# Two norms taken from raw halves of the residual, head sums in column tiles, and a reordered tail in a two-layer hybrid decoder kernel

## The chip, the cores and the metric

The kernel runs on one core of a Trainium2 chip. The metric is the device time of one execution in microseconds (us), lower is better. Time before: median of three runs.

## What is computed

Two decoder layers over 256 positions of width 1024, all in float32. What matters here, cut from the reference:

```python
def rmsnorm(x, g, eps=RMS_EPS):
    y = x * lax.rsqrt(jnp.mean(x * x, axis=-1, keepdims=True) + eps)
    return y * g

h = h + even_mixer(rmsnorm(h, ln_mix[0]), ...)        # norm 0
h = h + swiglu(rmsnorm(h, ln_ffn[0]), ...)            # norm 1
gate = sigmoid(rmsnorm(h, ln_ple[0]) @ w_ple_gate[0]) # norm 2
h = h + gate * (p[0] @ w_ple_proj[0])
hn = rmsnorm(h, ln_mix[1])                            # norm 3
proj = hn @ w_in_odd                                  # q, k, v, z, b, a
qkv = silu(causal_dwconv(qkv, conv_w))                # 4 taps
q, k = l2norm(q), l2norm(k)                           # per head of 128
beta, g = sigmoid(b), -exp(a_log) * softplus(a + dt_bias)
o = chunk_gated_delta_rule(q, k, v, g, beta)          # chunks of 64
h = h + (rmsnorm(o, onorm_g) * silu(z)) @ w_out
h = h + moe_swiglu(rmsnorm(h, ln_ffn[1]), ...)        # top 2 of 8
```

After the experts come a second gate stage and the final norm.

## The kernel before

One program for the whole trunk, with the order of every engine's work written out by hand and semaphores between the engines. Weights stream in pieces of 128x2048 float32 (1 MB): SyncE loads a piece into one of six `raw` slots, ScalarE (ACT) rounds it to `w_hi` (`split`, L1355), VectorE (DVE) forms the rest `w_lo` (L1906), and TensorE (PE) multiplies in three products, high by high, high by low, low by high (`product`, L593 to L595). Activations are split the same way into `xs_hi` and `xs_lo`. `w_hi` and `w_lo` have three slots, so the split of a piece waits until the third last one is used. `splits(n)` and `ahead_to(n)` in a program mean: split all pieces up to n here; everything behind such a call on that engine waits for it.

A norm (0 to 3) goes: ACT squares and sums the residual `h` and takes the root (`norm_std`, L1374, L1375), DVE takes the reciprocal and writes the scaled `hn` (`norm_hn`, L1924, L1925), PE transposes the 16 blocks of `hn` (`norm_x`, L656), ACT and DVE split them with the gain (`norm_hi` L1384, `norm_lo` L1930), and the following products start.

Around norm 2, PE finishes the down projection of the dense SwiGLU, runs `proj` for the embedding (24 matmuls), waits for norm 2 (`norm_x(2)`), and runs the gate matmuls (four pieces, 96 matmuls of 512 columns, `tokens_out`). ACT applies the sigmoid (L1524), DVE multiplies and adds to `h` (L2149, L2089), and norm 3 follows in the same way. Then comes the DeltaNet layer: `small_product` (L834) and `small_turn` (L843) for b and a; twelve pieces of q, k, v (`qkv`, 48 matmuls of 256 columns each, alternating between PSUM banks 0 and 1). ACT copies each bank into the padded `upo` (`pad`, L1558), DVE applies the four taps (`conv`, L2180 and L2182), ACT the SiLU. `decay_sums` (L932), `gram`, `x_first` and five levels of a block inversion (`level_p`, `level_x`, all L942) run between the pieces. `square` (ACT, L1550) and `l2_sum` (PE, L896: matmuls with one column, four for each of two heads and two token tiles, eight such calls with four matmuls each) give the squared norms of q and k; DVE's `head_squares` (L2198) reads them. Small results of PE share banks 2 and 3 in the order of the list `SIDE`; a step may start when the one two places ahead has been read (`side_bank`).

At the end of the inversion come `corner`, `z_unit` (12 matmuls of 512 columns each), u (L1057), w (L1062, read by ACT as `nwT`, L1654), `scores` (L918), the state (L1071), the outputs, the per-head norm (`head_squares` and `head_roots` on ACT, L1668 and L1672; `head_factors` and `head_scale` on DVE, L2371 and L2364), the transposes `heads_turn` (L1111), and the output projection (`P_OUT_O`), which reads them split by `heads_hi` (L1686) and `heads_lo` (L2390). Then router, experts (four pairs or more of 84 pieces each), last gate and final norm.

## Time and profile before

| | |
|---|---|
| median of 3 runs | 1662.44 us (1661.19 to 1668.97) |
| the profiled execution's own time | 1666.08 us |
| its span, first to last instruction | 1664.3 us |
| mean granted TensorE clock | 0.986 |
| busy PE / DVE / ACT | 1610.2 / 1321.5 / 1058.8 us |
| HBM read | 447.75 MB |

The trace has every instruction with its start, its length, and the engine that ended the idle time before it. Ends of matmuls are modelled, so lengths of one matmul overlap; starts are what to go by. The granted clock is the share of full speed (2.4 GHz) that TensorE was given: 1.00 or 0.50 (1.2 GHz), and values between where a stretch has both.

### The profile page before, as it was taken

The numbers are of one execution on the slowest core, as the hardware profiler recorded it, in microseconds if no ns is written. First come the engines' busy times: TensorE is split into PE (matmuls) and PEld (weight loads), VectorE is DVE, ScalarE is ACT, GpSimd is POOL, SyncE is SP. The second block draws the span as 40 slices with busy tenths as digits, with TensorE's granted clock in tenths as the row PEclk, the third lists the DMA queues.
The fourth block names the chain that finished last, engine by engine and source line by source line (L and its number), as shares of the span: only waits on it lengthen the run. The fifth ranks groups of instructions, "written<-read, shape, count | busy, mean of one in ns | idle before, by whom it ended". The sixth has DMA issues, their size and how long they took to land.

```text
span 1664.3 us, 21969 instructions
## 1 busy us (share of the span) xinstructions
PE 1610.2 (97%) x9012; PEld 1359.4 (82%) x9012; DVE 1321.5 (79%) x1175; ACT 1058.8 (64%) x940; POOL 28.4 (2%) x24
## 2 busy tenths in 40 slices
PE   7988999997999989999999999999999999999997
PEld 6977888886999877788888888888888888888885
DVE  5766666666687568888989889889889888889886
ACT  5554344336543258677777777777777777777777
POOL 0000000000131100000000000000000000000000
PEclk9999999999989999999999999999999999999999
DMA  9634555544323236999999999999999998999991
GB/s 299 205 104 158 203 177 202 178 152 127 102 79 102 76 138 210 336 367 372 359 367 326 369 363 381 347 377 326 371 376 369 356 368 302 380 366 358 362 372 41
DMA packets 220191, 450.22 MB, mean 271 GB/s; under 512 B 10270, under 2 KB 58300, under 8 KB 220092
## 3 DMA queue, kind: packets, MB, share of 16 engines
q1 hardware_dynamic: 219404, 447.78, 75.2%
q8 instruction: 71, 1.16, 0.3%
q10 hardware_dynamic: 688, 1.05, 0.2%
q14 instruction: 28, 0.23, 0.0%
HBM read 447.75 MB, written 1.05 MB: 270 GB/s over the span
## 4 chain that ended last, share of the span: by engine, by line
PE 89%; DVE 6%; ACT 3%; issue 1%; DMA 0%; SPq 0%; ACTq 0%; DVEq 0%
PE ps L593 24%; PE ps L594 23%; PE ps L595 23%; PE ps L774 6%; PE ps L776 3%; DVE w_lo L1906 2%; PE ps L942 2%; PE ps L637 1%; ACT w_hi L1355 1%; DVE odd L2182 1%; PE ps L896 0%; DVE h L2089 0%; ACT L1367 0%; PE ps L1214 0%; PE ps L1180 0%
## 5 line engine op out<-in xcount | busy, mean ns | idle before, releaser
L1906 DVE TENSOR_TENSOR w_lo<-raw,w_hi 128x2048 fp32r<-128x2048 f32 x421 | 960.6, 2297 | 192.5 <-ACT w_hi L1355 192.1
L1355 ACT ACTIVATE w_hi<-raw 128x2048 fp32r<-128x2048 f32 x421 | 806.4, 1917 | 226.7 <-PE ps L595 221.7
L593 PE MATMUL ps<-w_hi,x_both 128*128 128x512 f32 x1096 | 438.2, 400 | 14.5 <-DVE x_both L1930 8.2
L595 PE MATMUL ps<-w_hi,x_both 128*128 128x512 f32 x1096 | 430.7, 393 | 0.0
L594 PE MATMUL ps<-w_lo,x_both 128*128 128x512 f32 x1096 | 429.5, 392 | 0.0
L593 PEld LDWEIGHTS ps<-w_hi,x_both 128*128 128x128 f32 x1096 | 207.9, 190 | 59.8 <-issue 8.0
L595 PEld LDWEIGHTS ps<-w_hi,x_both 128*128 128x128 f32 x1096 | 207.3, 189 | 44.8
L594 PEld LDWEIGHTS ps<-w_lo,x_both 128*128 128x128 f32 x1096 | 208.2, 190 | 41.3
L594 PE MATMUL ps<-w_lo,ff 128*128 128x512 f32 x576 | 226.4, 393 | 0.0
L593 PE MATMUL ps<-w_hi,ff 128*128 128x512 f32 x576 | 226.2, 393 | 0.0
L595 PE MATMUL ps<-w_hi,ff 128*128 128x512 f32 x576 | 224.6, 390 | 0.0
L774 PE MATMUL ps<-x_both,w_hi 128*128 128x512 f32 x448 | 159.1, 399 | 0.4 <-DVE x_both L1930 0.4
L593 PEld LDWEIGHTS ps<-w_hi,ff 128*128 128x128 f32 x576 | 108.2, 188 | 24.3
L595 PEld LDWEIGHTS ps<-w_hi,ff 128*128 128x128 f32 x576 | 108.2, 188 | 23.9
L594 PEld LDWEIGHTS ps<-w_lo,ff 128*128 128x128 f32 x576 | 108.3, 188 | 21.7
L776 PE MATMUL ps<-x_both,w_lo 128*128 128x256 f32 x448 | 125.8, 281 | 0.0
L774 PEld LDWEIGHTS ps<-x_both,w_hi 128*128 128x128 f32 x448 | 84.2, 188 | 21.7 <-issue 0.6
L776 PEld LDWEIGHTS ps<-x_both,w_lo 128*128 128x128 f32 x448 | 84.7, 189 | 0.5
L593 PE MATMUL ps<-x_both,w_hi 128*128 128x256 f32 x288 | 84.9, 295 | 0.0
L594 PE MATMUL ps<-x_both,w_hi 128*128 128x256 f32 x288 | 82.5, 287 | 0.0
L595 PE MATMUL ps<-x_both,w_lo 128*128 128x256 f32 x288 | 82.4, 286 | 0.0
L1764 ACT ACTIVATE ff<-ps,ff 128x512 f32<-128x512 f32 x56 | 38.5, 688 | 41.8 <-PE ps L595 41.8
(332 smaller groups left out, 1262.5 us busy)
## 6 DMA issues: line engine op xcount, KB each, us to landing
raw<-in_w_moe SPq DMA_DIRECT2D x336, 1024.0 KB, 6.7
raw<-in_w_dense SPq DMA_DIRECT2D x42, 1024.0 KB, 5.0
raw<-in_w_in_odd SPq DMA_DIRECT2D x16, 1024.0 KB, 5.5
raw<-in_w_in_even SPq DMA_DIRECT2D x12, 1024.0 KB, 10.8
raw<-in_w_ple_gate SPq DMA_DIRECT2D x8, 1024.0 KB, 6.5
raw<-in_w_out_even SPq DMA_DIRECT2D x4, 1024.0 KB, 5.9
raw<-in_w_out_odd SPq DMA_DIRECT2D x4, 1024.0 KB, 5.0
raw<-in_w_ple_proj SPq DMA_DIRECT2D x2, 1024.0 KB, 4.8
```

The costliest lines, as they stand in the source:

```text
L593: pe.matmul(acc, lh, rh, start=first, stop=False)
L594: pe.matmul(acc, lh, rl, start=False, stop=False)
L595: return pe.matmul(acc, ll, rh, start=False, stop=final)
L637: last = pe.transpose(ps[:, bank, c * P:(c + 1) * P], src[:, c * P:(c + 1) * P], ident)
L774: pe.matmul(ps[:, 2 * m + c, :], wh[:, k, c * P:(c + 1) * P], x_both[:, k * 2 * SEQ:(k + 1) * 2 * SEQ], start=(k == 0), stop=False)
L776: last = pe.matmul(ps[:, 2 * m + c, 0:SEQ], wl[:, k, c * P:(c + 1) * P], xs_hi[:, k, :], start=False, stop=(k == KC - 1))
L942: last = pe.matmul(ps[rows, bank, cols], lhs(rows, hd, cols), rhs(rows, hd, cols), start=True, stop=True)
L1355: act.activation(w_hi[:, n % SPLIT, :], raw[:, slot, :], ACT.Copy).then_inc(hi_rdy, 1)
L1764: act.activation(sil[:, s % 2, :], ps[:, 2 * (s % 2), :], ACT.Silu, scale=gslot[:, u, 1:2]).then_inc(silu_sb, 1)
L1906: dve.tensor_tensor(w_lo[:, n % SPLIT, :], raw[:, slot, :], w_hi[:, n % SPLIT, :].bitcast(F32), ALU.subtract).then_inc(lo_rdy, 1)
L2182: last = dve.scalar_tensor_tensor(qkvT[:, ch, :], src, tap, qkvT[:, ch, :], ALU.mult, ALU.add)
```

## The change

1. **Norms 2 and 3.** PE transposes raw `h` in two halves of 512 columns (`turn_h`), the gain is applied in the split as before, and 1/rms is applied to the products. For norm 2 it is the `scale` of the sigmoid. For norm 3 it is a row `rb` (two matmuls broadcast `rstd` over the partitions, ACT copies it) that multiplies q, k, v as they leave PSUM, the `scale` of the SiLU of z, and a factor on b and a. ACT sums squares by halves (`half_square`), DVE adds eps (`half_eps`), `half_root` and `half_rstd` follow. `norm_std`, `norm_hn` and `norm_x` for these two are gone.
2. **Order around them.** The last down projection runs half by half (`mlp_half`), residual adds follow each half, `proj` is cut in two around the transposes, the gate's last piece runs behind `turn_h(3, 0)`, and the first q, k, v pieces start with the lower half of the inputs.
3. **Convolution.** `pad` goes from ACT to DVE (PSUM times `rb`), the first tap from DVE to ACT (`tap`).
4. **Squared sums.** Four calls for four heads each instead of eight for two: four matmuls with a stationary 128x32 of ones, each into 32 partitions of its own, 256 columns; ACT copies the result (`l2_out`), two transposes (`l2_turn`), DVE reads.
5. **Tail.** In the corner stage the split of `P_QKV_O + 15` moves behind the w copies on ACT; piece 17's split moves behind the second `head_roots` and `head_scale`; `heads_turn(1)` moves between the two token tiles of the first output piece.

```diff
@@ PE, last down projection and norm 2
-                for c in range(2):
-                    for t in range(NT):
-                        at = c * SEQ + t * P
-                        for half in range(2):
+                for half in range(2):
+                    for c in range(2):
+                        for t in range(NT):
+                            at = c * SEQ + t * P
...
+                    if s == HALF_FJ - 1 and half == 0:
+                        last.then_inc(mlp_half, 1)
...
-            norm_x(2)
+            pe.wait_ge(h_ready, H_AT[2][0])
+            turn_h(2, 0)
+            proj_e(0)
+            pe.wait_ge(h_ready, H_AT[2][2])
+            turn_h(2, 1)
+            proj_e(1).then_inc(piece_used, 1)
...
+            for j, half, t in ((0, 0, 0), (0, 0, 1), (0, 1, 0), (0, 1, 1)):
+                gate_e(j, half, t)
+            first(2, KC - 1)
+            gate_e(1, 0, 0)
+            gate_e(1, 0, 1)
+            pe.wait_ge(h_ready, H_AT[3][0])
+            turn_h(3, 0)
+            gate_e(1, 1, 0)
+            gate_e(1, 1, 1)
@@ PE, start of the DeltaNet layer
-            qkv(0)
+            split_wait(P_QKV_O)
+            pe.wait_ge(h_ready, H_AT[3][1])
+            small_product(3, 2, x_both, wba_s, 4 * HEADS_D, small_ps, range(0, 4))
+            qkv_part(0, 0, range(0, 4))
+            pe.wait_ge(sgm_sb, 2 * NT)
+            turn_h(3, 1, (0,))
+            pe.wait_ge(h_ready, H_AT[3][2])
+            turn_h(3, 1, (1,))
+            split_wait(P_QKV_O + 1)
+            qkv_part(1, 0, range(0, 4))
+            qkv_part(0, 0, range(4, KC))
+            small_product(3, 2, x_both, wba_s, 4 * HEADS_D, small_ps, range(4, KC))
+            qkv_part(0, 1, range(KC)).then_inc(piece_used, 1)
+            pe.wait_ge(rs_rdy, 2 * NT)
+            for t in range(NT):
+                last = pe.matmul(ps[:, 6, t * P:(t + 1) * P], rstd[:, 3, t:t + 1].broadcast_to([P, P]), ident,
+                                 start=True, stop=True)
+            last.then_inc(rb_ps, 1)
             pe.wait_ge(small_sb, 1)
             small_turn(0, 7, 4 * HEADS_D, C_S16, smallT_ps)
@@ PE, squared sums
-            def l2_sum(i):
-                bank = side_bank(("l2", i))
-                pe.wait_ge(l2_sq, i % 8 + 1 + (4 if i >= 8 else 0))
-                for t in range(NT):
-                    for c in range(2):
-                        last = pe.matmul(ps[:, bank, 2 * t + c:2 * t + c + 1],
-                                         sq[:, i % 2, c * SEQ + t * P:c * SEQ + (t + 1) * P], ones[:, 0:1],
-                                         start=True, stop=True)
+            def l2_sum(u):
+
+                bank = side_bank(("l2", u))
+                pe.wait_ge(l2_sq, 2 * u + 2)
+                if u == 0:
+                    pe.wait_ge(d_exp, 4)
+                for c in range(4):
+                    last = pe.matmul(ps[32 * c:32 * c + 32, bank, 0:SEQ], ones[:, 0:32],
+                                     squares_of(u)[c // 2][:, (c % 2) * SEQ:(c % 2 + 1) * SEQ], start=True, stop=True,
+                                     tile_position=(0, 32 * c))
+                last.then_inc(l2_ps, 1)
...
             qkv(4)
             l2_sum(0)
+            gram(0)
+            l2_turn(0)
             l2_sum(1)
-            gram(0)
-            l2_sum(2)
-            l2_sum(3)
             gram(1)
+            l2_turn(1)
@@ ACT, convolution and corner stage
-            def pad(i):
-
-                act.wait_ge(piece_used, P_QKV_O + i + 1)
-                if i >= 4:
-                    act.wait_ge(cv_done, i - 3)
-                act.activation(upo[:, i % 4, :, DN_TAPS - 1:], ps[:, i % 2, :].rearrange("p (c s) -> p c s", c=2),
-                               ACT.Copy).then_inc(q_pad, 1)
+            def tap(i):
+
+                act.wait_ge(q_pad, i + 1)
+                for m in range(2):
+                    ch = 2 * QKV_ORDER[i] + m
+                    last = act.activation(qkvT[:, ch, :], upo[:, i % 4, m, 0:SEQ], ACT.Copy, scale=cwT[:, ch:ch + 1])
+                last.then_inc(tap_sb, 1)
@@ DVE, convolution
+            def pad(i):
+
+                dve.wait_ge(piece_used, P_QKV_O + i + 1)
...
+                dve.tensor_tensor(upo[:, i % 4, :, DN_TAPS - 1:], ps[:, i % 2, :].rearrange("p (c s) -> p c s", c=2),
+                                  over(rb, 2), ALU.mult).then_inc(q_pad, 1)
@@ PE, first output piece
-            tokens_out((6, 7), (xs_hi, xs_lo), P_OUT_O, 0, ready_k=heads_in)
-            heads_turn(1)
+            for t in range(NT):
+                for k in range(4):
+                    heads_in(k)
+                    last = product(ps[:, 6 + t, :], (xs_hi[:, k, t * P:(t + 1) * P], xs_lo[:, k, t * P:(t + 1) * P]),
+                                   (wh[:, k, :], wl[:, k, :]), k == 0, False)
+                if t == 0:
+                    heads_turn(1)
```

How the order moves, at three places. The first is DVE behind the last down projection: before,

```order
L2130 TENSOR_TENSOR ff<-ps,ff 128x512 [waits pT_hi]
L1906 TENSOR_TENSOR w_lo<-raw,w_hi 128x2048 [waits hi_rdy]
L2089 TENSOR_TENSOR h<-h,ps 128x512 [waits piece_used]
L2089 TENSOR_TENSOR h<-h,ps 128x512 x3
L1924 RECIPROCAL rstd<-std 128x1 [waits n_std,h_ready]
L1925 TENSOR_SCALAR hn<-h,rstd 128x1024 [waits dve_link]
L1924 RECIPROCAL rstd<-std 128x1 [waits n_std]
L1925 TENSOR_SCALAR hn<-h,rstd 128x1024 [waits dve_link]
L1906 TENSOR_TENSOR w_lo<-raw,w_hi 128x2048 [waits hi_rdy] x2
```

and in the change:

```order
L2254 TENSOR_TENSOR ff<-ps,ff 128x512 [waits pT_hi]
L2030 TENSOR_TENSOR w_lo<-raw,w_hi 128x2048 [waits hi_rdy]
L2213 TENSOR_TENSOR h<-h,ps 128x512 [waits mlp_half]
L2213 TENSOR_TENSOR h<-h,ps 128x512
L2030 TENSOR_TENSOR w_lo<-raw,w_hi 128x2048 [waits hi_rdy]
L2213 TENSOR_TENSOR h<-h,ps 128x512 [waits piece_used]
L2213 TENSOR_TENSOR h<-h,ps 128x512
L2054 SCALAR_TENSOR_TENSOR x_both<-ps,gT,x_both 128x256 [waits n_hi] x4
```

Two of the four residual adds now come earlier than before, and a weight split stands between the two pairs. The second place is ACT in the corner stage (corner copies L1595 and L1716, squares L1550 and L1663, w copies L1654 and L1779): before,

```order
L1595 ACTIVATE raw<-ps 64x8x64 [waits corner_ps]
L1565 ACTIVATE odd<-odd 128x512 [waits cv_done]
L1550 ACTIVATE odd<-odd 128x512 [waits cv_silu,side_ps]
L1595 ACTIVATE raw<-ps 64x8x64 [waits corner_ps]
L1355 ACTIVATE w_hi<-raw 128x2048 [waits piece_used,raw_in2]
L1654 ACTIVATE odd<-ps 128x512 [waits w_ps] x2
L1565 ACTIVATE odd<-odd 128x512 [waits cv_done]
L1550 ACTIVATE odd<-odd 128x512 [waits cv_silu,side_ps]
```

and in the change:

```order
L1716 ACTIVATE raw<-ps 64x8x64 [waits corner_ps]
L1685 ACTIVATE odd<-odd 128x512 [waits cv_done]
L1716 ACTIVATE raw<-ps 64x8x64 [waits corner_ps]
L1663 ACTIVATE odd<-odd 128x512 [waits cv_silu,l2_ps]
L1685 ACTIVATE odd<-odd 128x512 [waits cv_done]
L1663 ACTIVATE odd<-odd 128x512 [waits cv_silu,l2_ps]
L1671 ACTIVATE s<-ps 128x256 [waits side_ps,l2_ps]
L1779 ACTIVATE odd<-ps 128x512 [waits w_ps] x2
L1434 ACTIVATE w_hi<-raw 128x2048 [waits piece_used,raw_in2]
```

The last squares move ahead of the w copies and the weight split behind them; on DVE the matching `w_lo` still stands ahead of the last `head_squares`. The third place is ACT at the head norms (roots L1672 and L1796): before,

```order
L1672 ACTIVATE osd<-oss 128x8 [waits od_sum]
L1668 ACTIVATE odd<-odd 128x1024 [waits od_sb]
L1355 ACTIVATE w_hi<-raw 128x2048 [waits piece_used,raw_in0]
L1672 ACTIVATE osd<-oss 128x8 [waits od_sum]
L1367 ACT_TABLE_LOAD
L1367 ACTIVATE eps<-eps 128x1
```

and in the change:

```order
L1796 ACTIVATE osd<-oss 128x8 [waits od_sum]
L1792 ACTIVATE odd<-odd 128x1024 [waits od_sb]
L1796 ACTIVATE osd<-oss 128x8 [waits od_sum]
L1446 ACT_TABLE_LOAD
L1446 ACTIVATE eps<-eps 128x1
L1434 ACTIVATE w_hi<-raw 128x2048 [waits piece_used,raw_in0,act_link]
```

The second root no longer has a weight split ahead of it, and the split follows the table load.

## Rows read from the trace of the kernel before

**Rows 1.** The page: busy time of each engine, and the costliest groups on DVE and ACT

```profile
PE 1610.2 (97%) x9012; PEld 1359.4 (82%) x9012; DVE 1321.5 (79%) x1175; ACT 1058.8 (64%) x940; POOL 28.4 (2%) x24
...
L1906 DVE TENSOR_TENSOR w_lo<-raw,w_hi 128x2048 fp32r<-128x2048 f32 x421 | 960.6, 2297 | 192.5 <-ACT w_hi L1355 192.1
L1355 ACT ACTIVATE w_hi<-raw 128x2048 fp32r<-128x2048 f32 x421 | 806.4, 1917 | 226.7 <-PE ps L595 221.7
```

**Rows 2.** Waits of PE from 300 to 700 us: total, times, longest

```profile
PE ps L656 <- DVE hn L1925: 5.3, 1, 5.3
PE ps L593 <- DVE x_both L1930: 4.2, 1, 4.2
PE ps L1111 <- DVE odd L2364: 3.1, 1, 3.1
PE ps L896 <- DVE yneg L2198: 2.1, 1, 2.1
PE ps L896 <- ACT odd L1550: 2.0, 1, 2.0
PE ps L834 <- DVE x_both L1930: 1.6, 1, 1.6
...
PE ps L593 <- DVE x_both L2390: 1.2, 1, 1.2
```

**Rows 3.** Windows: length, busy PE, PEld, DVE, ACT, POOL (instructions), granted clock, DMA share, GB/s

```profile
385.00:388.00 3.00, 3.00 (x9) 2.35 (x8) 2.97 (x3) 0.00 (x0) 0.00 (x0) 0.50 0.85 291
...
461.00:469.00 8.00, 8.00 (x61) 7.87 (x61) 5.17 (x12) 2.08 (x3) 1.83 (x2) 0.50 0.46 131
566.00:571.00 5.00, 5.00 (x23) 5.00 (x24) 1.10 (x4) 0.00 (x0) 1.01 (x1) 0.50 0.56 204
598.00:602.00 4.00, 1.11 (x9) 1.13 (x10) 2.71 (x6) 0.84 (x3) 0.00 (x0) 1.00 0.32 76
680.00:800.00 120.00, 120.00 (x543) 98.95 (x543) 106.96 (x63) 89.19 (x58) 0.00 (x0) 1.00 1.01 369
```

**Rows 4.** Timeline around norm 2: start us, length us, engine, line, operation, [idle before <-releaser]

```profile
369.01 2.29 DVE L1906 TENSOR_TENSOR w_lo<-raw,w_hi 128x2048 fp32r<-128x2048 f32 x1 [1.11 <-ACT w_hi L1355]
372.07 2.48 DVE L2089 TENSOR_TENSOR h<-h,ps 128x512 f32<-128x512 f32 x4 [0.77 <-PE ps L595]
...
377.37 1.80 PE L656 MATMUL ps<-con,hn 128*128 128x128 f32 x15
...
379.81 3.00 ACT L1384 ACTIVATE x_both<-ps,gT 128x256 fp32r<-128x256 f32 x8
```

**Rows 5.** Timeline on ACT at the end of the two gate halves, and behind them

```profile
396.35 1.09 ACT L1524 ACTIVATE hn<-ps 128x512 f32<-128x512 f32 x2 [2.01 <-PE ps L595]
...
407.23 1.09 ACT L1524 ACTIVATE hn<-ps 128x512 f32<-128x512 f32 x2 [3.43 <-PE ps L595]
408.33 1.28 ACT L1367 ACT_TABLE_LOAD   x1
```

**Rows 6.** Timeline, opening of the DeltaNet layer, up to the first level of the inversion

```profile
427.10 0.28 PE L843 MATMUL ps<-con,odd 32*128 32x16 f32 x1
...
439.90 0.60 ACT L1558 ACTIVATE odd<-ps 128x512 f32<-128x512 f32 x1 [3.36 <-PE ps L595]
...
440.45 2.71 DVE L2182 SCALAR_TENSOR_TENSOR odd<-odd,cwT 128x256 f32<-128x256 f32 x6
...
455.68 1.84 PE L896 MATMUL ps<-con,odd 128*128 128x1 f32 x16
...
478.86 1.10 PE L942 MATMUL ps<-odd 64*64 64x64 f32 x32
```

**Rows 7.** Timeline, corner stage: the second w copy on ACT, and the state's start on PE

```profile
563.49 0.60 ACT L1654 ACTIVATE odd<-ps 128x512 f32<-128x512 f32 x1 [0.30 <-PE ps L1062]
...
574.22 1.95 PE L1071 MATMUL ps<-odd 128*128 128x128 f32 x16
```

**Rows 8.** Timeline, head norms: the second root on ACT

```profile
597.04 0.19 ACT L1672 ACTIVATE osd<-oss 128x8 f32<-128x8 f32 x1
```

More of the change, by code:

```diff
@@ L1608, in _ @@
             act.activation(dcy[:, :, :, :], dcy[:, :, :, :], ACT.Exp).then_inc(dcy_rdy, 1)
-            decay(0, 0)
-            decay(0, 1)
-            pad(3)
-            decay(1, 0)
-            decay(1, 1)
+            for t in range(NT):
+                for g in range(2):
+                    decay(t, g)
             silu_conv(0)
             square(0)
+            tap(3)
             silu_conv(1)
```

352 lines of the change are left out of this document (221 added, 131 removed).

## The prediction

> **What bounds the kernel now.** I read the page first: PE is busy 97% of the span, DVE 79%, ACT 64% [rows 1]. So time can come only from PE: its waits, its slow-clock stretches, and work taken off it. The windows say that from 680 us on, in the experts, PE works every microsecond at full clock [rows 3]. The change touches nothing there, so the question is how much earlier PE reaches that stage. The waits of PE between 300 and 700 us say what can be won before it: 5.3 and 1.6 us at norm 3, 4.2 at norm 2, 2.1 and 2.0 at squared sums, 3.1 and 1.2 at the head norms, 19.5 us together [rows 2]. The windows add a second loss. Behind most of these waits PE was granted 0.50, which is 1.2 GHz, for a while: 3 us behind norm 2's, 8 us behind the first squared sums' and 5 us behind the last's [rows 3]. Work runs at half speed there, so these three cost 1.5, 4 and 2.5 us. Behind the 3.1 us wait the clock stayed at 1.00 [rows 3]: a wait does not always bring it down.
>
> **The change part by part.** I walk PE through the new order with durations of the rows and compare the time at five places with the time before. Units: a weight split is 1.9 us on ACT and 2.3 on DVE [rows 1]; 12 gate matmuls are 2.7, from 48 between the two sigmoids, 10.9 us [rows 5]; a transposed block is 0.12, so eight are 1.0 [rows 4]; a q, k, v piece is 5.85, from two of them between the turn that starts at 427.1 and takes 1.0, and 439.8 [rows 6]; a residual add is 0.62 [rows 4].
>
> *Norm 2.* Removed from the path: root, reciprocal, scaling and all 16 transposes between the last add and the split. Added: waits of PE for the adds. The down projection ends at about 372.0. The first two adds need its first half (over by 369.3) and DVE, which is free at 371.3 [rows 4], so they end at 372.6: PE waits 0.6, transposes until 373.6, and runs half of `proj` until 376.3. The second two adds stand behind a weight split on DVE, and that behind ACT, which first does two half squares (1.4, an estimate: 1024 columns at the rate of the 2048-column copy, and two reads of a sum) from 372.0 and then the split until 375.4. DVE splits until 377.7 and adds until 379.0. So PE waits 2.7 us, a new wait where there was none; then transposes (380.0), the other half of `proj` (382.8), gate. The gate started at 383.5 before (transposes from 377.4, 1.9, and the 4.2 us wait [rows 2, 4]): gain 0.7. Next is the second gate piece: ACT splits the inputs (0.38 a block [rows 4]) until 381.4, loads a table (1.3 [rows 5]), takes roots, splits the weights until 385.4, DVE until 387.7; PE wants it at 388.3. It is hidden by 0.6 us only.
>
> *Gate and norm 3.* Eight groups of 2.7 and the eight transposes in between end at 405.8, against 407.1 before: gain 1.3, of which 1.5 is the slow stretch that I leave out here. PE then waits for the product of the second sigmoid: ACT splits a piece until 403.6, DVE until 405.9, then sigmoid product and add, 407.3: a wait of 1.5. From there the lower halves of b, a and of two pieces cover the last transposes and splits, and the root comes after them. PE is at the small turn at 417.9 and waits for ACT (weight split, copy of `rb`, small copy) until 419.1. Before it was there at 427.1 [rows 6]: **gain 8.0**. With the parts of piece 1 already done, piece 2 starts at 424.8, not 433.9: 9.1.
>
> *Opening of the DeltaNet layer.* The decay gate comes 7.5 us earlier, at 424.0, through the same short chain with one more factor. From there DVE's chain to the third convolution is as long as before: `conv` loses two of its eight instructions (under 0.9 us) and keeps six at 2.7 [rows 6], `pad` adds one pass of 0.7 over 512 columns from PSUM, and a memset of 0.9 leaves. The tap on ACT has no row; a 128x256 block from PSUM is 0.38 [rows 4] and a 2048-column copy scaled down is 0.24, so two are 0.5 to 0.8. I take 0.8, since PSUM blocks are the nearer size. Queued behind `pad` on DVE are the weight splits, and behind `tap` on ACT its own: each pad waits for a DVE that is splitting. PE's next piece needs its bank freed, and in my walk it is, by 2 to 3 us each time. After piece 4 (446.5) PE waits 0.4 for squares and 1.6 for the fourth SiLU (449.1); the DVE chain then lets `x_first` start at 459.5 and level 1 at 464.8, against 478.9 [rows 6]: **gain 14.1**, with no slow clock in it.
>
> *Squared sums.* Eight calls fall away; two of them take 1.84 [rows 6], so 7.4 us. Four calls of four matmuls with 256 columns come, with two transposes each (0.24). No row has column tiles. A float32 matmul is two instructions, 128 columns of it 0.24; 256 columns are 0.46, four in turn 1.84, four side by side 0.46. The row of 64x64 tiles has 32 instructions of 64 columns in 1.1 us, 0.035 each [rows 6], where a transpose's rate would give 0.06, so tiles do overlap: I take 0.6 a call. Two calls were in the levels: 1.84 less 0.84, **gain 1.0** (bounds: 1.1 and a loss of 0.2).
>
> The Trainium skill ("TensorEngine Tiling (Array Packing)", Key Properties) says that different tiles can load and multiply in parallel, but also that a change of the tiling mode drains the engine. The first half agrees with the row of 64x64 tiles; the second speaks against this change, which enters and leaves column tiles four times. By the drain and no overlap the levels would lose 0.2 us instead of winning 1.0; no row here shows a drain.
>
> *Corner stage.* The 2.0 us wait for the last squares goes, with the slow 5 us behind it and 1.8 of work against 0.8. But the weight split now stands behind the w copies on ACT. These end at 564.1 [rows 7], about 563.6 in the same frame with the work saved. The split ends on ACT at 565.5 and on DVE at 567.8, and only then may `head_squares` read the sums, for which the second `scores` waits through its bank: 568.2. PE had come there at 564, so it waits 4 us: the late split is what comes last next. Scores (1.0) and a z unit (2.8) follow, the state starts at 572.0 instead of 574.2 [rows 7]: **gain 2.2**.
>
> *Head norms.* The second root starts at 597.0 [rows 8], and the split next to it kept DVE from the factor until 599.4 (ACT's part ends at 597.1, DVE's 2.3 later). Without it the root is at 596.4 and the factor at 596.8, 2.6 us earlier: the 3.1 us wait shrinks to 0.5. The split comes to lie ahead of `heads_hi` and `heads_lo`, which makes PE wait 1.1 before the first output piece. `heads_turn(1)` inside that piece removes the wait of 1.2. **Gain 2.6.**
>
> *Sum:* 14.1 + 1.0 + 2.2 + 2.6 = 19.9 us at full clock. New waits of 2.7, 1.5, 1.6 and 4 us remain; most like them were followed by a slow clock [rows 3]. I take three such stretches, at 3, 4 and 5 us long (the rows have 3, 8 and 5, but ACT and DVE cover part where they are the later ones), 6.0 us. That leaves 13.9. The profiled execution took 1666.1, so it would take 1652.2; its 1666.1 is 3.6 above the median of the runs, and against the median of 1662.4 the forecast is **1648.5 us**.
>
> **The rivals.**
> A. *The clock stays up*, as it did behind the 3.1 us wait. Then the 19.9 come whole: 1642.5. Against it: three other waits of 2 to 4 us. Chance 0.18.
> B. *The waits only move.* Splits queued ahead of adds, pads and sums make DVE and ACT the bound. From the small turn's 8.0 on nothing more is won in the opening, the slow clock costs 3.4 around the gate and the corner is even; the head norms keep 1.3: about 6 us, 1656.5. For it: three places with slack under 1 us in my walk, and DVE at 79%. Chance 0.20.
> C. *The levels lose their pace; slower.* `pad` now stands on DVE ahead of the `update` that the next level waits for. If DVE falls over 2 us a level behind, PE waits in each of five levels, and each wait brings about 8 slow microseconds like those at 461 us [rows 3], 4 us lost: 5 x 6 = 30 less 14, so 1678. Against it: a level takes PE some 13 us, and DVE gets only 0.1 more per level. Chance 0.05.
> D. *The experts don't start earlier.* Their loads run at 1.01 of the DMA engines [rows 3]; were they the bound, an earlier PE would wait there: 1662. Against it: PE has no gap from 680 on, and the loads are released by the splits, which move with PE. Chance 0.05.
>
> **How the numbers follow.** The forecast with its 13.9 holds 0.52. A measurement of this kernel tells 0.5%, 8.3 us, from no change. Faster by more: forecast, A and a fifth of B, 0.74. Within: the rest of B and D, 0.21. Slower: C, 0.05. The range 1641 to 1659 holds A, the forecast with a tap, a tile or a slow stretch at its other bound, and most of B; outside lie C, D and the edge of B, some 0.15.
>
> **What would show it.** In the new profile: L656's 5.3 us wait and the two waits at L896 gone; waits of 2 to 3 us at the second half's transposes of norm 2 and of about 4 at the second scores; the small turn near 419, level 1 near 465 to 468; column tile calls of 0.5 to 1 us; experts of unchanged length. I am wrong if level 1 is not at least 8 us earlier, if the levels take longer than before, or if the slow clock takes over 10 us in the stage.

## The result, and the profile after

| | before | after |
|---|---|---|
| median of the runs made together, 6 each | 1662.78 us (1661.03 to 1668.97) | 1654.75 us (1651.40 to 1655.37) |
| the profiled execution's own time | 1666.08 us | 1651.40 us |
| its span | 1664.3 us | 1649.6 us |
| mean granted clock | 0.986 | 0.989 |

The ratio is 0.994, with a 95% interval from 0.9924 to 0.9957. The forecast was 1648.5 with a range of 1641 to 1659: faster, as measured, but by 13.9 us where the medians give 8.0. The two profiled spans lie 14.7 apart, which looks like the forecast come true. It is not quite that: before's profiled execution is 3.3 us above the median of these runs and after's is the fastest of its six, and, as the experiments show, 3.2 us of the 14.7 come from an address, which the prediction did not see at all.

In the changed kernel the code has new line numbers: the products are L601 to L603 (before L593 to L595), `w_lo` L2030, `w_hi` L1434, `turn_h` L654, `add_h` L2213, `small_product` L869, the squared sums L941 and their transposes L951, `gram` and levels L995, `scores` L971, DVE's `head_squares` L2344, `pad` L2335, `conv` L2316, `xt_first` L2393, the heads' transposes L1183. The page after, to be read beside [rows 1]: PE lost 12.9 us of busy time, DVE 5.7.

```profile
PE 1597.3 (97%) x8992; PEld 1347.8 (82%) x8992; DVE 1315.8 (80%) x1164; ACT 1065.9 (65%) x964; POOL 27.3 (2%) x24
```

The waits of PE from 300 to 700 us, in total, times, longest, beside [rows 2]. The 5.3 us at L656 and both at L896 are gone (0.7 is left at L941, which does the squared sums now), and of the 3.1 at the heads 0.3 is left. New are 3.8 at the second scores, 2.5 at the second half's transposes (the prediction had 4 and 2.7), 1.5 at b and a (L869; the prediction had 1.5 there), three shorter ones at `gram`, `x_first` and level 1 (L995), and a wait for a DMA:

```profile
PE ps L971 <- DVE yneg L2344: 3.8, 1, 3.8
PE ps L654 <- DVE h L2213: 3.5, 3, 2.5
PE ps L995 <- DVE odd L2393: 1.8, 1, 1.8
PE ps L995 <- ACT odd L1685: 1.7, 1, 1.7
...
PE ps L869 <- issue: 1.5, 1, 1.5
PE ps L768 <- DMA ff<-in_ln_final: 1.3, 1, 1.3
...
PE ps L995 <- ACT odd L1705: 0.7, 1, 0.7
```

How early PE is at the places of the prediction, from the timelines. The forecast column has the sum at full clock; the 6.0 us for the slow clock were to come off at the end.

| place | before, us | forecast, us | after, us | earlier by | forecast gain |
|---|---|---|---|---|---|
| gate of norm 2 | 383.5 | 382.8 | 384.5 | -1.0 | 0.7 |
| small turn | 427.1 | 419.1 | 420.8 | 6.3 | 8.0 |
| level 1 | 478.9 | 464.8 | 471.0 | 7.8 | 14.1 |
| state | 574.2 | 556.9 | 565.4 | 8.8 | 17.3 |
| router's sums (L1165, now L1244) | 639.7 | 625.8 with the slow clock | 629.8 | 9.9 | 13.9 |
| end of the span | 1664.3 | | 1649.6 | 14.7 | 13.9 |

So PE reached the router 4 us later than forecast, and 4.8 us more of gain appeared behind it, in a part that was to stay as it was. The windows tell where the clock was down (columns as in [rows 3]; the lost time of a window is 10 us times what its clock lacks to 1.00). Of the kernel before:

```profile
380.00:390.00 10.00, 6.52 (x22) 5.24 (x23) 7.97 (x11) 4.61 (x9) 0.00 (x0) 0.83 0.46 118
410.00:420.00 10.00, 5.99 (x23) 3.93 (x23) 7.89 (x15) 7.46 (x15) 0.00 (x0) 0.77 0.29 79
420.00:430.00 10.00, 10.00 (x74) 9.72 (x74) 0.62 (x4) 2.93 (x5) 0.00 (x0) 0.89 0.17 61
460.00:470.00 10.00, 9.29 (x66) 9.16 (x67) 7.17 (x15) 3.08 (x3) 2.83 (x2) 0.50 0.37 105
560.00:570.00 10.00, 7.98 (x52) 7.82 (x52) 4.61 (x6) 4.23 (x5) 0.01 (x1) 0.78 0.40 140
570.00:580.00 10.00, 10.00 (x59) 8.90 (x58) 2.08 (x3) 1.19 (x2) 4.67 (x4) 0.88 0.00 0
660.00:670.00 10.00, 7.79 (x31) 5.92 (x30) 9.52 (x26) 6.16 (x5) 0.00 (x0) 0.90 0.70 245
670.00:680.00 10.00, 10.00 (x42) 8.13 (x41) 7.88 (x6) 5.75 (x3) 0.00 (x0) 0.93 0.98 352
```

That is 15.2 us. After, the windows below 1.00 from 370 to 680 us hold 6.8:

```profile
370.00:380.00 10.00, 6.89 (x34) 5.31 (x34) 7.11 (x8) 6.00 (x12) 0.00 (x0) 0.95 0.00 0
380.00:390.00 10.00, 10.00 (x44) 8.42 (x43) 5.38 (x13) 9.00 (x14) 0.00 (x0) 0.88 0.01 3
...
450.00:460.00 10.00, 8.85 (x111) 7.78 (x112) 6.28 (x15) 6.90 (x10) 1.62 (x2) 0.83 0.01 2
460.00:470.00 10.00, 8.20 (x99) 7.74 (x99) 9.90 (x11) 1.42 (x3) 5.99 (x3) 0.83 0.36 107
560.00:570.00 10.00, 9.83 (x57) 8.98 (x58) 2.95 (x7) 1.19 (x2) 3.46 (x3) 0.83 0.34 105
```

The 1.7 us lost before at 660 to 680 are one part of what appeared behind the router. The rest is found in the last experiment.

### The profile page after: what moved, and what is told of

It reads as the page before. It is cut to its first block, busy times and chain, and to the rows that moved or that the text cites. A ratio compares the mean times of both kernels' runs of the same rounds, so it can differ in the third digit from the quotient of the medians.

```text
span 1649.6 us, 21944 instructions
## 1 busy us (share of the span) xinstructions
PE 1597.3 (97%) x8992; PEld 1347.8 (82%) x8992; DVE 1315.8 (80%) x1164; ACT 1065.9 (65%) x964; POOL 27.3 (2%) x24
## 4 chain that ended last, share of the span: by engine, by line
PE 84%; DVE 8%; ACT 5%; issue 2%; DMA 1%; SPq 0%; ACTq 0%; DVEq 0%
PE ps L601 22%; PE ps L603 22%; PE ps L602 22%; PE ps L782 6%; DVE w_lo L2030 4%; PE ps L784 3%; PE ps L995 2%; ACT w_hi L1434 2%; PE ps L645 1%; ACT L1446 1%; DVE h L2213 0%; DMA ff<-in_ln_final 0%; DVE odd L2316 0%; PE ps L1293 0%; ACT x_both L1463 0%
## 5 line engine op out<-in xcount | busy, mean ns | idle before, releaser
L2030 DVE TENSOR_TENSOR w_lo<-raw,w_hi 128x2048 fp32r<-128x2048 f32 x421 | 960.7, 2297 | 195.3 <-ACT w_hi L1434 194.9
L1434 ACT ACTIVATE w_hi<-raw 128x2048 fp32r<-128x2048 f32 x421 | 806.4, 1917 | 211.8 <-PE ps L603 208.6
L601 PE MATMUL ps<-w_hi,x_both 128*128 128x512 f32 x1096 | 437.3, 399 | 10.6 <-DVE x_both L2054 4.2
L603 PE MATMUL ps<-w_hi,x_both 128*128 128x512 f32 x1096 | 429.8, 392 | 0.0
L601 PEld LDWEIGHTS ps<-w_hi,x_both 128*128 128x128 f32 x1096 | 207.4, 189 | 55.3 <-issue 6.7
L603 PEld LDWEIGHTS ps<-w_hi,x_both 128*128 128x128 f32 x1096 | 206.9, 189 | 44.5
L601 PE MATMUL ps<-w_hi,ff 128*128 128x512 f32 x576 | 225.9, 392 | 0.0
L603 PE MATMUL ps<-w_hi,ff 128*128 128x512 f32 x576 | 224.8, 390 | 0.0
L603 PEld LDWEIGHTS ps<-w_hi,ff 128*128 128x128 f32 x576 | 108.3, 188 | 23.0
L601 PEld LDWEIGHTS ps<-w_hi,ff 128*128 128x128 f32 x576 | 108.5, 188 | 22.4
L601 PE MATMUL ps<-x_both,w_hi 128*128 128x256 f32 x288 | 84.6, 294 | 0.1
L603 PE MATMUL ps<-x_both,w_lo 128*128 128x256 f32 x288 | 82.0, 285 | 0.0
L1888 ACT ACTIVATE ff<-ps,ff 128x512 f32<-128x512 f32 x56 | 38.6, 689 | 41.2 <-PE ps L603 41.2
```

Source lines behind the costliest of these rows:

```text
L601: pe.matmul(acc, lh, rh, start=first, stop=False)
L603: return pe.matmul(acc, ll, rh, start=False, stop=final)
L1434: act.activation(w_hi[:, n % SPLIT, :], raw[:, slot, :], ACT.Copy).then_inc(hi_rdy, 1)
L1888: act.activation(sil[:, s % 2, :], ps[:, 2 * (s % 2), :], ACT.Silu, scale=gslot[:, u, 1:2]).then_inc(silu_sb, 1)
L2030: dve.tensor_tensor(w_lo[:, n % SPLIT, :], raw[:, slot, :], w_hi[:, n % SPLIT, :].bitcast(F32), ALU.subtract).then_inc(lo_rdy, 1)
```

## The experiments

All were timed beside the kernel before, in four sets, and a ratio is to the kernel before of the same set. Its median was 1664.14 us in the first set (after_again, sums_first, adds_first, before_filled), 1663.54 in the second (both_first, level_first, tail_only, before_filled2), 1663.28 in the third (level_first2, tail_first, best2) and 1664.47 in the fourth (before_shift). A ratio comes from all executions and can differ a little from that of the two medians. after_again, level_first, level_first2 and tail_first lie within each other's intervals, so the times do not tell these four apart and only the profiles do; sums_first and adds_first, timed in the same set as after_again, just touch its interval, and both_first and best2 are clear of it.

| run | base | median us | ratio | 95% interval |
|---|---|---|---|---|
| after_again | changed | 1652.58 | 0.9929 | 0.9915 to 0.9944 |
| sums_first | changed | 1647.82 | 0.9904 | 0.9886 to 0.9922 |
| adds_first | changed | 1648.27 | 0.9914 | 0.9897 to 0.9931 |
| both_first | changed | 1643.30 | 0.9871 | 0.9856 to 0.9887 |
| level_first | changed | 1650.23 | 0.9917 | 0.9904 to 0.9930 |
| level_first2 | changed | 1651.82 | 0.9931 | 0.9918 to 0.9945 |
| tail_first | changed | 1651.01 | 0.9924 | 0.9910 to 0.9938 |
| best2 | changed | 1636.81 | 0.9853 | 0.9839 to 0.9866 |
| before_filled | before | 1664.60 | 1.0001 | 0.9991 to 1.0010 |
| before_filled2 | before | 1661.07 | 0.9980 | 0.9971 to 0.9988 |
| tail_only | before | 1662.43 | 0.9986 | 0.9975 to 0.9997 |
| before_shift | before | 1662.17 | 0.9983 | 0.9972 to 0.9994 |

**The changed kernel once more (after_again).**

> The changed kernel once more, beside the kernel before on the same chip. Theory 1 (waits and slow clock): in the two profiled executions the change took 14.7 us off, of which 8.4 is slow clock that happened to differ (lost to half speed in 10 us windows: 21.4 us before, 15.3 after, over the whole span; 15.2 and 6.8 from 370 us on). So the medians differ by less than the profiles: 6 to 11 us, ratio 0.9935 to 0.996, and the time lost to the slow clock in a new profile is 8 to 16 us. Theory 2 (the experts start no earlier in most executions): the medians differ by under 5 us, and the end of the new profile lies under 8 us ahead of the old one.

The same kernel gave 1652.58 here and 1654.75 in the runs of the result; its waits are the same to 0.1 us, while its profiled execution lost 10.2 us to the slow clock from 370 to 680 us, not 6.8. So the waits repeat and the clock does not: two profiles of one kernel lie 3.4 us apart there by the clock alone. The following runs on the changed kernel are held against 1652.6.

**The squares' wait in the corner (sums_first).** DVE reads the last squared sums ahead of the split, not behind it:

```diff
@@ DVE, corner stage
-            ahead_to(15)
             head_squares(3)
+            ahead_to(15)
```

> The changed kernel, but DVE reads the last squared sums before it splits the piece whose high part now comes late. Theory 1 (the 3.8 us wait at the second scores is the DVE order, and costs in full): the wait is gone, the state starts 3.8 to 5.5 us earlier (5.5 with the slow clock behind it), median 3 to 6 us under the changed kernel's. Rival (the late weight split itself then holds the z units): the wait goes to a z unit, median within 1.5 us of the changed kernel's.

The corner of the changed kernel, PE and then DVE (start us, length us): the sums are in PSUM at 555.4, but DVE waits 4.3 us for ACT's half of the split, splits until 559.9 and only then reads them. This is the wait that the prediction had walked out, down to its size.

```profile
555.05 0.38 PE L951 MATMUL ps<-con,s 128*128 128x128 f32 x2
555.27 1.06 PE L971 MATMUL ps<-odd 128*128 128x128 f32 x8
560.17 2.08 PE L971 MATMUL ps<-odd 128*128 128x128 f32 x8 [3.84 <-DVE yneg L2344]
```

```profile
557.68 2.29 DVE L2030 TENSOR_TENSOR w_lo<-raw,w_hi 128x2048 fp32r<-128x2048 f32 x1 [4.29 <-ACT w_hi L1434]
559.89 0.22 DVE L2344 TENSOR_SCALAR yneg<-ps 128x4 f32<-128x4 f32 x2
```

In sums_first DVE reads them at 553.07 and the scores run through; from the small turn to the state PE takes 139.2 us instead of 144.6. The median fell by 4.8 us: the wait of 3.8 and about 1 us of the slow clock behind it (the 560 window is at 0.83 above, which is 1.7 us in that one execution, and at 1.00 in sums_first).

```profile
552.87 1.95 PE L971 MATMUL ps<-odd 128*128 128x128 f32 x16
```

**The adds' wait at norm 2 (adds_first).** DVE adds the second halves of the residual ahead of the split of the gate piece:

```diff
@@ DVE, norm 2
-            splits(P_GATE_E)
             dve.wait_ge(piece_used, P_PROJ_E)
             for t in range(NT):
                 add_h(t, 1, ps[:, 5 + 2 * t, :]).then_inc(h_ready, 1)
+            splits(P_GATE_E)
```

> The changed kernel, but DVE does the second pair of residual adds of norm 2 before the weight split. Theory 1 (the 2.5 us wait before the second half's transposes is the split that stands ahead of the adds): that wait is gone and the gate starts 3 to 4 us earlier; about 1 us comes back as a wait for the second gate piece, whose split follows the norm on ACT; median 2 to 3.5 us under the changed kernel's. Rival (the weight split of the second gate piece becomes the bound): the gain is under 1 us.

After: the second transposes wait 2.47 us and then run at half speed (1.97 us for what takes 1.07 in the row above it). In adds_first they start at 376.87 without a wait, the gate starts at 380.5 instead of 384.5, and a wait of 0.47 us comes at the second gate piece, the one that the prediction had as covered by 0.6 us only. 4.3 us less in all.

```profile
373.11 1.07 PE L654 MATMUL ps<-con,h 128*128 128x128 f32 x8 [0.64 <-DVE h L2213]
379.40 1.97 PE L654 MATMUL ps<-con,h 128*128 128x128 f32 x8 [2.47 <-DVE h L2213]
```

**Both together (both_first).**

> The changed kernel with both reorderings of the two runs before it: DVE reads the last squared sums ahead of the split of piece 15, and adds the second residual halves of norm 2 ahead of the split of the gate piece. Alone they measured 4.8 and 4.3 us under the changed kernel. Theory 'two waits in series, each paid in full': 1652.6 - 4.8 - 4.3 = 1643.5 us (1642 to 1645). Rival 'the time gained at norm 2 is taken back by the squares' wait or by the loads': the better of the two alone, 1647.8 us.

1643.3 us, where 1643.5 was expected: two waits in series on PE, each paid in full.

**Filling the waits of the kernel before (before_filled, before_filled2).** PE runs matmuls that nothing reads while it waits at norm 3, at the third squared sums and at the last ones, so that the engine is not idle ahead of the stretches with the slow clock. They add work to the program and take none away.

```diff
+            def fill(bank, n):
+                for _ in range(n):
+                    pe.matmul(ps[:, bank, :], ident, con[:, 0:512], start=True, stop=True)
...
+            pe.wait_ge(h_ready, H_AT[3][0] - 1)
+            fill(0, 11)
...
+            pe.wait_ge(d_exp, 4)
+            fill(6, 4)
...
+            pe.wait_ge(u_sb, 2)
+            fill(4, 4)
```

> The kernel before, with matmuls that nothing reads put into three waits of TensorE: 11 of 128x512 float32 before the transposes of norm 3, 4 before the third squared sum, 4 before the last one. Nothing else is changed, and no wait gets shorter. Theory 1 (the slow clock comes from the waits and costs half the time it lasts): the granted clock stays at 1.00 behind these three waits, and the kernel gains what they cost in the profile, 3.4 + 5 + 3.4 less what another engine takes back, 5 to 11 us. Rival (the clock falls for another cause, such as the kind of work): no gain, or a loss of up to 1 us.

The fills were too long: one of these matmuls takes 0.87 us, so 11 of them took 9.6 us in a wait of 5.3, and 4 of them 3.5 in waits of 2.1 and 2.0. The clock did stay at 1.00 in all three stretches, and the median was that of the kernel before (ratio 1.0001). In the profiled execution the sum closes: about 12 us less of slow clock up to 680 us (3.4 against 15.2), some 7 us of overrun, and the router's sums 5.0 us earlier. But this execution, at 1661.15 us, was the fastest of twelve, and the median shows no such gain. With 5, 2 and 2 of them:

> The kernel before with unread matmuls in the same three waits as the filled kernel before it, now 5, 2 and 2 of them, at 0.87 us each 4.4, 1.7 and 1.7 us, which is no more than the waits last. Theory 'the slow clock behind the waits costs': the granted clock stays at 1.00 in the three stretches, and the 12 us that the profile of the kernel before loses there (3.4 at 404 to 430, 5 at 460, 3.4 at 560 to 580) come back as far as the executions timed have them too: 5 to 12 us under 1664.1, so 1652 to 1659. Rival 'behind a slow PE the others catch up, so full speed only lengthens the next wait': 0 to 2 us, 1662 to 1664. Third case: the clock falls in spite of the fills, since they are float32 and short, and the time is 1664.

Here the fill at norm 3 takes 4.45 us and fits. The result lies between the theories: 1661.07, a ratio of 0.9971 to 0.9988, so 2.0 to 4.8 us, where 5 to 12 were expected. The clock was not kept up everywhere; in this profile it was down at the norm 2 wait, which had no fill, and again behind two of the fills:

```profile
380.00:390.00 10.00, 5.94 (x16) 4.75 (x17) 8.56 (x11) 5.20 (x10) 0.00 (x0) 0.66 0.41 112
410.00:420.00 10.00, 6.24 (x27) 2.97 (x25) 7.85 (x14) 8.48 (x17) 0.00 (x0) 0.97 0.31 89
420.00:430.00 10.00, 10.00 (x68) 8.90 (x68) 1.80 (x8) 1.94 (x3) 0.00 (x0) 0.85 0.28 93
460.00:470.00 10.00, 9.81 (x84) 8.55 (x83) 9.02 (x16) 4.07 (x5) 3.71 (x3) 0.83 0.38 107
```

So the slow clock does cost time, some microseconds, but not each microsecond that one profile shows as lost. How much of it belongs to a given wait these runs do not settle.

**The opening of the levels (level_first, level_first2).** Level 1 came 6.2 us later than forecast. The first run takes DVE's `xt_first(0)` ahead of a split and ACT's copy `x_first(0)` ahead of `tap(5)`, which had held ACT for 8.6 us; the second moves `x_first(1)` there as well.

```diff
@@ DVE
-            ahead_to(6)
             xt_first(0)
+            ahead_to(6)
             xt_first(1)
@@ ACT (level_first2; level_first moves only the first copy)
+            x_first(0)
+            x_first(1)
             tap(5)
-            x_first(0)
             ahead_to(8)
             silu_conv(4)
-            x_first(1)
```

> The changed kernel; at the opening of the levels DVE makes the first transposed block (xt_first(0)) ahead of the split of piece 6, and ACT copies the first product (x_first(0)) ahead of tap(5), which had to wait 8.6 us for a pad that stands behind a convolution. Theory 'order of the opening': PE's 1.8 us wait before x_first(0) and its 0.7 us wait before level 1 go, and with them about 1.5 us lost in the slow clock behind the first; level 1 starts at 467 instead of 471.0, and the kernel takes 1649 to 1650 (3 to 4 us under 1652.6). Rival 'DVE beside GpSimd': DVE's six instructions of conv(4) take 4.7 us instead of 2.7 while GpSimd's masks run, so everything behind them on DVE stays where it is, PE waits in level 1 instead and the time is 1652 to 1653.

> The run level_first once more, with ACT's second copy (x_first(1)) ahead of tap(5) as well. In level_first PE's wait before x_first(0) was gone, but a wait of 2.1 us came before the second half of level 1, released by the copy of x_first(1), which had stood behind tap(5) and a split on ACT. Theory 'ACT's queue': that wait goes too, 1650.2 - 2.1 = 1648.1 us, the state starts about 2 us earlier than the 563.8 of level_first. Rival 'DVE is the bound of the opening, behind GpSimd's masks': the wait comes back under DVE's name in the first level, 1650 us.

The first median, 1650.2, is where the first theory had it, and the theory is wrong all the same. In that profile the state comes 145.1 us behind the small turn, no sooner than after's 144.6; what is earlier is the small turn itself, by 2.1 us, at a place that the edit does not touch. The named waits go, but 2.1 us come back at the second half of level 1, and when that copy is moved too, 0.98 and 1.00 come back in the levels and 0.76 at a split; that run has 1651.8, slower and not 2.1 faster.

In level_first2 level 1 starts 47.0 us behind the small turn instead of 50.2, the end of the levels (L1104) 116.1 instead of 117.1, and the state 144.6, as after. So of the 3.2 us won at level 1 some 2.2 are given back in the levels, and the last 1.0 in a longer slow stretch behind the corner's wait (the windows at 550 and 560 are at 0.84 and 0.82, after at 1.00 and 0.83). What gives them back is seen on ACT: the level's copy (L1711), for which PE waits, stands behind a tap and a split, and the tap waited 4.04 us for DVE's `pad`. ACT, then PE:

```profile
478.10 0.91 ACT L1678 ACTIVATE odd<-odd,cwT 128x256 f32<-128x256 f32 x2 [4.04 <-DVE odd L2335]
478.92 1.89 ACT L1434 ACTIVATE w_hi<-raw 128x2048 fp32r<-128x2048 f32 x1
480.72 0.57 ACT L1711 ACTIVATE odd<-ps 128x512 f32<-128x512 f32 x1
```

```profile
481.44 3.01 PE L995 MATMUL ps<-odd 64*64 64x64 f32 x96 [1.00 <-ACT odd L1711]
```

And DVE had little room to come sooner: it is busy 28.0 of 30 us in the changed kernel (24.4 in the same window of the kernel before, 26.4 from 463 to 493 us, around its own first levels), and 29.1 in level_first2. That DVE sets the pace here is read from these rows and not shown by a run of its own, and an order of ACT with these taps behind the level's copies was not tried. After, then level_first2:

```profile
455.00:485.00 30.00, 27.46 (x424) 26.29 (x421) 28.04 (x39) 15.67 (x19) 10.23 (x6) 0.94 0.36 107
```

```profile
455.00:485.00 30.00, 27.26 (x447) 26.10 (x447) 29.13 (x40) 15.25 (x20) 10.77 (x7) 1.00 0.36 107
```

Part of that busy time is stretch. Where GpSimd (POOL) masks the blocks, DVE's instructions stretch, and GpSimd's too. After, DVE's conv(4) takes 4.74 us for six instructions and the next one 3.62, against 2.71 in [rows 6]; GpSimd's mask takes 3.24 us beside DVE's split, and 1.30 two microseconds earlier beside a DVE product with one operand in PSUM. DVE first, then POOL:

```profile
457.49 1.38 DVE L2382 TENSOR_TENSOR raw<-ps,odd 64x512 f32<-64x512 f32 x2
...
464.00 4.74 DVE L2316 SCALAR_TENSOR_TENSOR odd<-odd,cwT 128x256 f32<-128x256 f32 x6
```

```profile
457.65 1.30 POOL L2007 TENSOR_TENSOR odd<-raw,con 128x512 f32<-128x512 f32 x1 [28.12 <-DVE raw L2388]
459.68 3.24 POOL L2007 TENSOR_TENSOR odd<-raw,con 128x512 f32<-128x512 f32 x1 [0.72 <-DVE raw L2388]
463.55 3.07 POOL L2007 TENSOR_TENSOR odd<-raw,con 128x512 f32<-128x512 f32 x2 [0.63 <-DVE odd L2393]
```

The Trainium skill ("SBUF — State Buffer", Who interferes with whom) says that a DVE instruction with two SBUF inputs contends with a GpSimd one that reads SBUF, and one with at most one SBUF input, outside DVE's 2-port modes, does not. The trace agrees with both halves, by the 4.74 and the 1.30 us. The kernel before had the same collision (there two first taps, L2180, take 2.68 us beside a mask, against 0.35 for one alone at 452.69 us), but behind a `qkv` piece at half speed, where PE waited for none of it. No run keeps the masks and DVE apart, so what the collision costs the changed kernel is not shown.

**The heads (tail_only, tail_first).** The change's order at the head norms alone, in the kernel before:

```diff
@@ ACT and DVE
-            ahead_to(17)
             head_roots(1)
             load_table(ACT.Silu)
+            ahead_to(17)
...
-            ahead_to(17)
             head_factors(1)
             head_scale(1, 0)
+            ahead_to(17)
@@ PE: heads_turn(1) between the two token tiles of the first output piece
```

> The kernel before with nothing but the change's order at the head norms: piece 17's split behind the second root and head_scale, heads_turn(1) between the two token tiles of the first output piece. Theory: 2.6 us of PE's waits of 3.1 and 1.2 go, 1664.1 - 2.6 = 1661.5 us, ratio 0.998; the second heads' waits in the profile are 0.3 to 0.5. Rival 'the split's 2.3 us come back ahead of the output piece': 1663.5 to 1664.1.

1662.43 us, 1.1 below by the medians; the ratio, 0.9986, gives 2.3, with an interval of 0.5 to 4.2. The profile splits it: from the state to the heads' transposes 24.0 us instead of 26.7, the 2.7 gained as predicted; from there to the router's sums 40.4 instead of 38.8, so 1.6 is lost again. The 1.2 us ahead of an output piece have only moved, and a wait for the load of `p_tok` is new:

```profile
594.69 1.06 PE L1111 MATMUL ps<-con,odd 128*128 128x128 f32 x8 [0.34 <-DVE odd L2371]
599.72 0.47 PE L593 MATMUL ps<-w_hi,x_both 128*128 128x512 f32 x1 [1.20 <-DVE x_both L2397]
613.10 0.66 PE L760 MATMUL ps<-con,ff 128*128 128x128 f32 x4 [1.29 <-DMA ff<-in_ln_final]
```

That row names `in_ln_final`, which ACT loads right behind `p_tok` and with the same semaphore. ACT issues both once DVE has split the last heads. PE now reaches its use sooner, the load does not. tail_first repairs both in the changed kernel:

```diff
@@ ACT
             heads_hi(1)
-            act.wait_ge(odT_lo, 4)
             act.dma_start(p_tok[:, :, :], a["p"][1, 0].rearrange("(t p) d -> p t d", p=P)).then_inc(p_in, 16)
             act.dma_start(gfin[:, :], a["ln_final"].unsqueeze(0).broadcast_to([P, D])).then_inc(p_in, 16)
+            act.wait_ge(odT_lo, 4)
@@ DVE
-            ahead_to(17)
             heads_lo(0)
             head_scale(0, 1)
             head_scale(1, 1)
-            ahead_to(18)
+            ahead_to(17)
             heads_lo(1)
+            ahead_to(18)
```

> The changed kernel with two repairs at the head norms: DVE rounds the first heads (heads_lo(0)) and the second ones ahead of the splits of pieces 17 and 18, and ACT issues the load of p_tok right behind heads_hi(1) instead of behind DVE's last heads_lo. Theory: the change's order moved the second transposes ahead but left the load where it was relative to DVE, so the 1.3 us that PE waits for it is new, and the 1.2 us before the first output piece are the split's; both go: 1652.6 - 2.4 = 1650.2 us, and from heads_turn to the gather 41.3 us instead of 43.7. Rival 'the splits that now come later, or the loads themselves, take their place': 1652.6 us and 43.7.

Both waits are gone and heads to gather takes 41.2 us, as expected. The median fell by 1.6 to 1651.0, less than 2.4; by time alone it is not clear of after_again (0.9910 to 0.9938 against 0.9915 to 0.9944).

**Everything together (best2).**

> All reorderings together on the changed kernel: squares ahead of a split, adds ahead of a split, the opening of the levels as in level_first2, the heads as in tail_first. If the waits stand in series and each is paid in full: 1643.3 - 4.5 (opening) - 2.4 (heads) = 1636.4 us. If the opening's gain is taken back once the corner no longer waits for the squares: 1641.

1636.81 us, ratio 0.9853 (0.9839 to 0.9866): 15.8 us better than the changed kernel (after_again) and 26.5 better than the one before. Its opening window:

```profile
455.00:485.00 30.00, 27.25 (x493) 25.93 (x493) 29.18 (x35) 12.21 (x18) 10.15 (x7) 1.00 0.38 110
```

DVE is as full here as in level_first2. The median is where the theory had it, but the theory's 4.5 us for the opening is not what the profiles show. The span is 8.0 us shorter than both_first's. Of these 1.5 are there before the gate of norm 2, where the two kernels are the same; 2.4 are the heads', from the state to the gather; 1.5 lie behind the gather, where both_first alone had a slow stretch (its 620 window is at 0.83). The other 2.7 lie between the small turn and the state (139.2 and 136.5 us). 1.7 of them is a slow stretch of both_first at 460 to 480 us, which followed a wait of 2.2 us for ACT's `x_first` copy (L1705) that best2 does not have. So the order of the opening gave between 1.0 and 2.7 us here, where in level_first2 it had given nothing by the state. With one profile of each, more cannot be said.

**An address (before_shift).** What remained was 3 us in the experts. The mean lengths of their matmuls differ in a group that the change does not touch, the down projection, whose stationary operand is a tensor of the expert stage (`ff`); of their operands it is the only one that stands behind the changed buffers in the order of allocation. From 700 to 1600 us, before and after:

```profile
L594 PE MATMUL ps<-w_lo,ff 128*128 128x512 f32 x409 | 160.9, 393 | 0.0
L593 PE MATMUL ps<-w_hi,ff 128*128 128x512 f32 x409 | 160.7, 393 | 0.0
L595 PE MATMUL ps<-w_hi,ff 128*128 128x512 f32 x409 | 159.0, 389 | 0.0
```

```profile
L603 PE MATMUL ps<-w_hi,ff 128*128 128x512 f32 x412 | 160.4, 389 | 0.0
L601 PE MATMUL ps<-w_hi,ff 128*128 128x512 f32 x411 | 160.3, 390 | 0.0
L602 PE MATMUL ps<-w_lo,ff 128*128 128x512 f32 x411 | 160.0, 389 | 0.0
```

The change makes two small buffers larger for its new sums, and every tensor allocated behind them moves up by 64 bytes. The experiment does that alone:

```diff
-        ssh = sb("ssh", [P, 3, NT, 2])
-        epsh = sb("epsh", [P, 3, NT])
+        ssh = sb("ssh", [P, 5, NT, 2])
+        epsh = sb("epsh", [P, 5, NT])
```

> The kernel before with two small buffers sized as in the changed kernel (ssh 5 instead of 3 norms, epsh too), which moves every tensor of the stages behind them 64 bytes up and changes nothing else. In the experts' down projection, where the stationary operand is one of these tensors, the three matmuls of a product take 393, 393 and 389 ns in every profile of the kernel before and its variants, and 390, 389 and 389 in every one of the changed kernel's: 448 x 7 ns = 3.1 us that neither the waits nor the clock explain. Theory 'the address': the changed kernel's lengths appear here, and from the gather to the end the kernel takes 1016.5 to 1018 us instead of 1019.6 to 1021.3; the time is 3 us under the kernel before, ratio 0.998. Rival 'something else of the change in the tail': 393 ns stay, ratio 1.000.

```profile
L593 PE MATMUL ps<-w_hi,ff 128*128 128x512 f32 x414 | 161.4, 390 | 0.0
L595 PE MATMUL ps<-w_hi,ff 128*128 128x512 f32 x413 | 160.8, 389 | 0.0
L594 PE MATMUL ps<-w_lo,ff 128*128 128x512 f32 x413 | 160.7, 389 | 0.0
```

The changed kernel's lengths appear. The two profiles happen to be as good a pair as one can have: the same windows at the same clocks up to 680 us, the gather at 643.0 and 643.1, and the ends at 1664.3 and 1661.1. The medians say 2.3 us, ratio 0.9983 (0.9972 to 0.9994). The other profiles agree: 393 or 394 ns in the first two rows of every kernel without the shift (before, before_filled, before_filled2, tail_only), 389 or 390 in every one with it. So 2 to 3 of the 8 to 12 us that the change brings are a gift of the allocator.

## Why the prediction was right, and where it was not

- **Direction and place: right.** Waits and slow stretches of PE between 370 and 640 us were what could be won, and the experts followed PE, still without a gap. Rival D has no support: in best2 the gather starts 14.7 us earlier than after, and the span ends 14.7 us earlier. Rival C (the levels lose their pace) did not happen either (from level 1 to their end 66.9 us, before 67.1), though DVE turned out very full there. Rival B (the waits only move) was right in part: it kept 1.3 us of the heads and none of the opening beyond the small turn, and 1.2 and 1.5 were measured. At the router the gain of 9.9 us lies halfway between B's 6 and the forecast's 13.9.
- **Norm 2 and the corner: right in mechanism and size.** Waits of 2.7 and 4 us forecast, 2.5 and 3.8 measured, behind exactly the splits that were named. What the prediction left out was the price of the first one's slow clock at its own place: the second transposes and `proj` ran at half speed, so the gate began 1.0 us later, not 0.7 earlier. These 1.7 us are also all that the small turn was late by (420.8 for 419.1). Levels and corner together brought the state 1.0 us, with 3.2 forecast: 1.7 of the rest is the slow stretch behind the 3.8 us wait, and the levels won 0.3 instead of 1.0.
- **The step that failed: the opening, 14.1 us.** Level 1 came 7.8 us earlier, and the prediction had named less than 8 as a sign that it is wrong. The opening was summed at full clock and with DVE's chain "as long as before". By the windows 5.1 us of the missing 6.2 are slow clock up to there (the forecast had put its 6.0 us at the end of the sum, so this part is no miss of the total), and about 1.1 is the chain itself. But level_first2 shows that the two do not simply add: without the slow window at 460 us, 1.7 us, the end of the levels came only 1.0 sooner. What stands behind it in the rows is the chain from DVE's `pad` over ACT's tap and split to the level's copy, with DVE busy 28 of 30 us from 455 to 485 and its conv(4) stretched beside GpSimd; that this chain is the cause is argued from the rows and not shown. Before, that collision was hidden, and the walk took its lengths from a place without it.
- **Column tiles: right.** A call takes 0.64 us (0.6 forecast, bounds 0.46 and 1.84), against 0.92 for each of twice as many before [rows 6]. The next matmul starts 0.56 us behind the first, so tiles ran side by side. The Trainium skill ("TensorEngine Tiling (Array Packing)", Key Properties) says that a change of the tiling mode drains the engine; these rows show no drain, and the levels did not lose the 0.2 us of that rival.

```profile
552.60 0.64 PE L941 MATMUL ps<-odd,con 128*32 128x256 f32 x8
553.16 2.05 PE L1134 MATMUL ps<-raw,odd 128*128 128x128 f32 x16
```

- **Head norms, 2.6 us: mis-sized, 1.2.** The walk ended at the output piece. The load of `p_tok`, issued behind the work that the order delays, was late next: the walk had counted the splits that move, and not this load.
- **The slow clock, 6.0 us: about right.** From 370 to 630 us both profiled executions of the changed kernel lost 6.8, and up to 680 us 6.8 and 10.2, before 15.2. As the largest unsteady term it sets how far a single profile can be trusted.
- **"Experts of unchanged length": wrong by 3.2 us**, by the address. This and before's slow stretch at 660 us made up what was missing at the router, 3.2 + 1.7 against 4.0 us. The close agreement of 13.9 with 14.7 is therefore luck in part. By medians the forecast gain was too high by 2.3 us in the repeat (1664.1 to 1652.6 is 11.6) and by 5.9 in the runs of the result (8.0). Without the 2.3 to 3.2 us of the address, 4.8 to 9.3 us are left for what the prediction reasoned about, so its sum was some 5 to 9 us too high; the range would have held without the address too (1654.75 + 3.2 is 1658).
- **Not taken apart.** Only the tail was run alone. How the rest of the gain divides among norms, convolution and squared sums is read from the profiles, and no run swaps `pad` and tap back.

## What to carry to other kernels

A split, a load or any bulk step that stands ahead of a small read on an in-order engine can be paid in full by whoever waits for that read: moving two such steps gave 9.3 us here, about as much as the whole change. When waits on the main engine are removed, add up how busy its suppliers are in that very window before adding up the gain. And compare the mean lengths of instructions that a change does not touch; if they differ, look at what moved in memory before giving the change the credit.

## What the runs showed that was not expected

- The address of the stationary operand, moved by 64 bytes, changes a 512-column matmul from 393 to 389 or 390 ns; over 448 products of three matmuls in the experts this is 3.2 us. Which boundary matters the runs do not tell: one shift was tried.
- DVE beside GpSimd: 4.74 us for six instructions that take 2.71 alone, 3.38 for a split that takes 2.28 (level_first), and 3.24 for a GpSimd mask that takes 1.30.
- A float32 matmul of 512 columns takes 0.87 us: it is two instructions of 0.43. This is why the first fills overran.
- The same waits of about 2 us were followed by 0.50 of the clock in one execution and by 1.00 in another (tail_only: no slow window from 480 to 1650 us, with the 2.0 us wait for the last squares still there).
